# One transformer-like block on one core: both mixer gates and the attention branch's product by seven products of half sums, token-major

## The chip, the cores and the metric

The kernel runs on one core of a Trainium2 chip. A core has TensorE (PE, matrix products into PSUM), VectorE (DVE), ScalarE (ACT), GpSimd (POOL) and SyncE (SP, which here issues DMAs). The metric is the device time of one launch in microseconds; lower is better. The time of the kernel before is the median of three runs.

## The reference

One block over 512 tokens of width 2048, all in fp32. `u = rms_norm(x)`; `proj = u @ w_in` is split into the recurrence's input and gate, q, k, v, the indexer's queries, keys and weights, and two mixer gates of 2048 columns each.

```python
xc = causal_depthwise_conv(rx, conv_w[l], conv_b[l])
ya = rg_lru(xc, w_rg_r[l], b_rg_r[l], w_rg_i[l], b_rg_i[l], lru_lambda[l]) * jax.nn.gelu(rgate)
yb = dsa_sparse_attention(q, k, v, iq, ik, iw, slopes)      # 8 heads, 128 selected keys of 512
mixed = (jax.nn.sigmoid(gate_a) * (ya @ w_branch_rnn[l])
         + jax.nn.sigmoid(gate_b) * (yb @ w_branch_attn[l]))
h = h + mixed @ w_out[l]
h = h + jnp.square(jax.nn.relu(rms_norm(h, norm_mlp_g[l]) @ w_mlp_up[l])) @ w_mlp_down[l]
```

`rg_lru` makes two sigmoid gates r and i from block-diagonal products, a = exp(-8 r softplus(-lambda)), and scans h = a h + sqrt(1 - a^2) i xc along the tokens. `ya` has 1024 channels, `yb` 1024. w_in has 2048 rows, w_branch_rnn and w_branch_attn 1024, w_out 2048.

## The kernel before

Every product is made from two parts of each operand: hi (a cast to fp32r, ACT) and lo (the rest, DVE), and three matmuls: hi times hi, hi times lo, lo times hi (`products`, L1905). Weights come in units of 1 MB (4 chunks of 128 rows by 512 columns) into two `raw` slots (SP), ACT casts a unit into `whi[slot]` (`hi`, L743), DVE makes `wlo[slot]` (L1250), and PE multiplies it: 4 quarters of 12 matmuls, 48 in all. `next_hi` and `next_lo` stand at the place of unit j and make the parts of unit j + 1; the cast can start when unit j - 1 has been multiplied, since it takes that unit's slot. Each engine has its own program in a fixed order, and semaphores tie them: `quarter` counts PE's quarters, `drained` the banks that were emptied, `lo_ready` the units that are ready.

The order of the stages on PE is: the normalised input u turned feature-major (`uhi`, `ulo`), 16 units IQRX (indexer queries and the recurrence's input, in two rounds i of 8 units; the first four of a round, j = 0 to 3, take 384 columns, and in the last four the index scores are made beside them: `idx_step` on PE, `relu_step` on ACT, scores on DVE), 8 units RG (the recurrence's gate, beside which DVE selects the keys), 16 units GA (gate A, feature-major, in a loop of four), 8 units WR (the recurrence's product), 8 units HD (the values), 16 units KQ (keys and queries of two heads at a time, with the attention of the pair before), 24 units GB (gate B, 16 units, and the attention branch's product, 8 units), 16 units WO (`w_out`), and the MLP. In the MLP both products are made by seven products of half sums instead of eight: token halves, row chunks taken alternately and column halves make three 2 by 2 matrices, `A11 B11, S1 T1, S2 T2, A12 B21, S3 T3, S4 B22, A22 T4`, each in two parts hf of 12 matmuls (down stage: `dhi`, `dlo` hold seven parts, L1183 and L1837; results are added to `hh` by DVE, L1762, or by ACT into `dn_tmp`, L1144, and POOL, L704).

The recurrence runs beside GA, one quarter of its channels per round of four units (46.4 us): DVE makes the convolution (L1396, L1401) in place of unit 0, the block-diagonal product (`lru_gates`) stands behind unit 1 on PE, ACT makes r, i, a, tanh (L863 to L870) and the root (L874), DVE the scan (L1427) and the product with the gate (L1430), ACT and DVE its parts (L877, L1433), and DVE `bdlo` (L1406). GA's results are copied to `mix` (L881), scaled by POOL (L645), put through the sigmoid (L849), multiplied by the recurrence's product (L1444); gate B and the branch's product are added at L1549 to L1565.

## Time and profile before

| | |
|---|---|
| median of 3 runs | 2568.51 us (2568.38 to 2568.74) |
| profiled execution, first to last instruction (span) | 2566.7 us |
| PE busy | 2550.2 us, 99% of the span |
| DVE, ACT, POOL busy | 1729.9, 1162.2, 437.8 us |
| PE's granted clock, mean | 0.999 of full speed |
| chain that ended last | PE 97%, DVE 1% |

The profiled execution has no time of its own beside its span; the median of the runs is 1.8 us above the span. A row of the page or of an answer names the line, the engine, what is written and read, the number of instructions, and their busy time. PE's matmuls overlap in the records: a 512-column matmul is shown as 390 ns long, while the next starts about 227 ns later, so PE's pace is read from counts in a stretch and not from busy time.

### The profile page before, as it was taken

What the parts mean: (1) busy time and instruction counts of PE and PEld (TensorE: products, weight loads), DVE (VectorE), ACT (ScalarE), POOL (GpSimd) and SP (SyncE); (2) the same over time, 40 slices, a digit from 0 to 9 for tenths busy, and PEclk for the clock granted to TensorE, in tenths of its full rate; (3) what the DMA queues carried; (4) which work ended last, traced back from release to release, by engine and by line L of the source; (5) the groups of instructions that cost most, each with busy time, mean ns of one, the idle gap of its engine ahead of it and who ended that gap; (6) DMA issues with size and microseconds to landing.
All of it is one profiled execution on the core that took longest, in us unless ns stands there. A gap on an engine that the chain in (4) does not pass through costs nothing.

```text
span 2566.7 us, 35536 instructions
## 1 busy us (share of the span) xinstructions
PE 2550.2 (99%) x13299; PEld 2199.0 (86%) x13299; DVE 1729.9 (67%) x1859; ACT 1162.2 (45%) x1455; POOL 437.8 (17%) x341
## 2 busy tenths in 40 slices
PE   9999999999999999999999999999999999999998
PEld 8888888888888888888889999999998888888886
DVE  5558765432355433342488888888888899999997
ACT  6332454411233322232366666566655555554545
POOL 1000121100000000000001211112111353443433
PEclk9999999999999999999999999999999999999999
DMA  5222233222322222234336655666568786545652
GB/s 196 85 99 96 84 100 100 96 86 97 99 82 82 66 99 98 98 115 151 130 119 202 207 184 188 205 205 199 184 195 322 278 245 246 180 168 213 239 213 83
DMA packets 244731, 393.53 MB, mean 153 GB/s; under 512 B 8848, under 2 KB 148720, under 8 KB 236848
## 3 DMA queue, kind: packets, MB, share of 16 engines
q1 hardware_dynamic: 238880, 378.17, 43.8%
q0 software_dynamic: 5520, 14.16, 2.1%
q8 instruction: 50, 0.82, 0.1%
q10 hardware_dynamic: 256, 0.18, 0.0%
q14 instruction: 25, 0.20, 0.0%
HBM read 325.24 MB, written 67.11 MB: 153 GB/s over the span
## 4 chain that ended last, share of the span: by engine, by line
PE 97%; DVE 1%; ACT 0%; POOL 0%; issue 0%; DMA 0%; ACTq 0%; DVEq 0%
PE stream L1910 16%; PE stream L1909 16%; PE stream L1911 16%; PE stream L2250 4%; PE stream L2252 4%; PE stream L2251 4%; PE aux L2250 4%; PE aux L2252 4%; PE aux L2251 4%; PE aux L2222 4%; PE stream L2222 3%; PE aux L2229 2%; PE aux L2227 2%; PE aux L2228 2%; PE stream L2229 2%; PE stream L2227 2%
## 5 line engine op out<-in xcount | busy, mean ns | idle before, releaser
L1250 DVE TENSOR_TENSOR wlo<-raw,whi 128x2048 fp32r<-128x2048 f32 x112 | 260.8, 2328 | 419.5 <-ACT whi L743 419.3
L743 ACT CAST whi<-raw 128x2048 fp32r<-128x2048 f32 x112 | 213.8, 1909 | 536.5 <-PE stream L1911 536.0
L1909 PE MATMUL stream<-uhi,whi 128*128 128x512 f32 (+1 forms) x1152 | 442.6, 384 | 0.0
L1910 PE MATMUL stream<-ulo,whi 128*128 128x512 f32 (+1 forms) x1152 | 441.5, 383 | 0.0
L1911 PE MATMUL stream<-uhi,wlo 128*128 128x512 f32 (+1 forms) x1152 | 441.4, 383 | 0.0
L704 POOL TENSOR_TENSOR hh<-hh,dn_tmp 128x512 f32<-128x512 f32 x112 | 220.7, 1991 | 328.0 <-ACT dn_tmp L1144 328.0
L1911 PEld LDWEIGHTS stream<-uhi,wlo 128*128 128x128 f32 x1152 | 216.2, 188 | 40.2
L1909 PEld LDWEIGHTS stream<-uhi,whi 128*128 128x128 f32 x1152 | 216.3, 188 | 39.3
L1910 PEld LDWEIGHTS stream<-ulo,whi 128*128 128x128 f32 x1152 | 216.3, 188 | 39.0
L1183 ACT CAST dhi<-d 128x1024 fp32r<-128x1024 f32 x160 | 167.7, 1053 | 164.1 <-PE aux L2252 99.4
L1837 DVE TENSOR_TENSOR dlo<-d,dhi 128x1024 fp32r<-128x1024 f32 x160 | 225.8, 1428 | 13.0 <-ACT dhi L1183 12.9
L2250 PE MATMUL stream<-dhi,dsum 128*128 128x512 f32 x448 | 174.5, 389 | 1.4 <-DVE hh L1762 0.9
L2252 PE MATMUL stream<-dhi,dsum 128*128 128x512 f32 x448 | 174.4, 389 | 0.2 <-issue 0.2
L2251 PE MATMUL stream<-dlo,dsum 128*128 128x512 f32 x448 | 174.3, 389 | 0.0
L2251 PE MATMUL aux<-dlo,dsum 128*128 128x512 f32 x448 | 174.3, 389 | 0.0
L2250 PE MATMUL aux<-dhi,dsum 128*128 128x512 f32 x448 | 174.3, 389 | 0.0
L2252 PE MATMUL aux<-dhi,dsum 128*128 128x512 f32 x448 | 174.3, 389 | 0.0
L660 POOL DMA_DIRECT2D h<-in_x x4 | 3.1, 771 | 776.7 <-DVE mix L1565 649.3
L1065 ACT CAST uwhi<-up_a 128x1024 fp32r<-128x1024 f32 x94 | 98.8, 1051 | 67.9 <-DVE up_a L1650 67.0
L1837 DVE TENSOR_TENSOR dlo<-dn_e,dhi 128x1024 fp32r<-128x1024 f32 x64 | 94.5, 1496 | 34.4 <-ACT dhi L1183 34.4
L1671 DVE TENSOR_TENSOR uwlo<-up_a,uwhi 128x1024 fp32r<-128x1024 f32 x94 | 114.2, 1215 | 0.0
L1671 DVE TENSOR_TENSOR uwlo<-up_b,uwhi 128x1024 fp32r<-128x1024 f32 x64 | 78.3, 1223 | 47.3 <-ACT uwhi L1065 47.3
(369 smaller groups left out, 6118.9 us busy)
## 6 DMA issues: line engine op xcount, KB each, us to landing
raw<-in_w_in SPq DMA_DIRECT2D x80, 1024.0 KB, 5.1
d<-in_w_mlp_down SPq DMA_DIRECT2D x64, 1024.0 KB, 8.3
dsum<-sums_d SPq DMA_DIRECT2D x56, 1024.0 KB, 11.8
up_b<-in_w_mlp_up SPq DMA_DIRECT2D x32, 1024.0 KB, 11.4
up_a<-in_w_mlp_up SPq DMA_DIRECT2D x32, 1024.0 KB, 9.8
sums_d<-hlo SPq DMA_DIRECT2D x32, 896.0 KB, 4.3
sums_d<-hhi SPq DMA_DIRECT2D x32, 896.0 KB, 7.3
raw<-in_w_out SPq DMA_DIRECT2D x16, 1024.0 KB, 5.1
```

The source lines that it names most:

```text
L704: pool.tensor_tensor(v, v, dn_tmp[r][:], ALU.add).then_inc(s.dn_p, 1)
L743: nc.scalar.copy(whi[slot][:, 0:width], raw[slot][:, 0:width]).then_inc(s.hi_ready, 1)
L1250: V.tensor_tensor(wlo[slot][:, 0:width], raw[slot][:, 0:width], whi[slot][:, 0:width].bitcast(F32), ALU.subtract).then_inc(s.lo_ready, 1)
L1671: V.tensor_tensor(uwlo[k][:], parts[j], uwhi[k][:].bitcast(F32), ALU.subtract).then_inc(s.up_lo, 1)
L1837: V.tensor_tensor(dlo[m % 7][:], parts[j], dhi[m % 7][:].bitcast(F32), ALU.subtract).then_inc(s.dn_lo, 1)
L1909: T.matmul(dst, ah, bh, start=first and k == 0, stop=False)
L1910: T.matmul(dst, ah, bl, start=False, stop=False)
L1911: ins = T.matmul(dst, al, bh, start=False, stop=last and k == n - 1)
L2222: ins = T.matmul(both(q), wh, both_parts(q, j), start=opens and q == 0, stop=q == KP - 1, skip_group_check=True)
L2250: T.matmul(dst, sh, wh, start=opens and i == 0, stop=False, skip_group_check=not opens)
L2251: T.matmul(dst, sh, wl, start=False, stop=False, skip_group_check=not opens)
L2252: ins = T.matmul(dst, sl, wh, start=False, stop=i == 3, skip_group_check=not opens)
```

## The change

PE no longer multiplies GA and GB. The order of the units is IQRX, RG, HD, KQ, WR, then ten gate steps, then WO. In the steps `st` 0 to 3 are gate A (two groups g of 1024 input rows, for two halves n of 1024 columns), 4 and 5 the attention branch's product, 6 to 9 gate B; each has the seven products in 14 parts m, of 12 matmuls each, with sums of tokens stationary and 512 weight columns moving. Weight sums are made on DVE (8 additions of 128x1024 a step), hi parts on ACT, lo parts on DVE, in a ring of five buffers (`GATE_RING`). Results are scattered into `acc_g` and `acc_r` (512 columns at a time, 14 pairs of halves): of the group that opens a sum, products 0, 1, 2, 6 by ACT (`gate_out`) and the rest by DVE (`gate_sum`); of the other group all by DVE.

The sums of tokens of u are made during IQRX: POOL adds the parts and makes four differences (`ur`, `us`), ACT and DVE split them (`ushi`, `uslo`, `u_sums_hi`, `u_sums_lo`, one of eight pairs k at each of the units 4 to 11), and POOL writes them to DRAM (`usum_d`); SP reads them back before the steps. The same is done with yb during WR (`ysum_d`, four pairs p of two heads; ACT and DVE wait for the spill of the pair before).

The recurrence (quarters i, `lru_*`) stands beside the values: one quarter per two HD units, the last one in the first KQ round. Some of it changes engines: the first tap and a^2 go to ACT, the product with the gate and `bdlo` to POOL; the values are now emptied by ACT (L1122 of the changed kernel) and not by DVE. WR is token-major, its four results go to `acc_r`; `rx`, `yahi` lose the 4 columns of padding.

Gate A's half n is multiplied by POOL (128x2048 at a time), written to DRAM (`mixa_d`), and added back to the attention half by an accumulating DMA of 1 MB from POOL's queue. The mixed rows are then turned feature-major on PE (`turn_mix`: 16 chunks, 64 transposes of 128x128), positions 0 to 7 within step 9, 8 to 15 within the first WO units, where ACT and DVE make `mhi` and `mlo`.

ACT's order in the index part, second round, before: the casts of the weight units 1 to 4 and then of the next one. `whi_51`, `whi_52` are the two slots; `iq` the queries' parts.

```order
L743 CAST whi_52<-raw_50 128x2048
L743 CAST whi_51<-raw_49 128x2048
L743 CAST whi_52<-raw_50 128x2048
L825 CAST iq<-stream 64x384 x8
L743 CAST whi_51<-raw_49 128x2048
```

The same place in the changed kernel; `ushi` are the split token sums.

```order
L942 CAST whi_52<-raw_50 128x2048
L1018 CAST ushi<-us 128x1024
L942 CAST whi_51<-raw_49 128x2048
L1018 CAST ushi<-us 128x1024
L942 CAST whi_52<-raw_50 128x2048
L1030 CAST iq<-stream 64x384 x8
L1018 CAST ushi<-us 128x1024
L942 CAST whi_51<-raw_49 128x2048
```

A cast of token sums now stands behind each cast of a weight unit, and the queries' casts have one behind them.

ACT's order beside the recurrence before, one round of gate A from its fourth unit's cast: `bdhi`, `yahi` parts for the block-diagonal product, `lru_*` the recurrence, `mix` gate A.

```order
L743 CAST whi_52<-raw_50 128x2048
L857 CAST bdhi<-bd 128x512
L860 CAST yahi<-lru_xc 128x512 x2
L863 ACTIVATE lru_rr<-aux,par 128x512 x2
L865 ACTIVATE lru_ii<-aux,par 128x512 x2
L868 ACT_TABLE_LOAD
L868 ACTIVATE lru_aa<-lru_rr,sp_t 128x512 x2
L870 ACTIVATE lru_th<-lru_rr,sp_t 128x512 x2
L743 CAST whi_51<-raw_49 128x2048
L874 ACT_TABLE_LOAD
L874 ACTIVATE lru_rr<-lru_th 128x512 x2
L877 CAST yahi<-lru_xc 128x512 x2
```

The changed kernel, from the exponentials of quarter 0 to the first tap of quarter 2 (`xc_80`, `xc_81` are the two convolution buffers, `vv` the values):

```order
L1088 ACTIVATE lru_aa<-lru_rr,sp_t 128x512 x2
L1091 ACTIVATE lru_th<-lru_rr,sp_t 128x512 x2
L1094 ACTIVATE lru_rr<-lru_aa 128x512 x2
L1099 ACT_TABLE_LOAD
L1099 ACTIVATE lru_rr<-lru_th 128x512 x2
L1069 CAST bdhi<-bd 128x512
L1072 CAST yahi<-xc_81 128x512 x2
L942 CAST whi_52<-raw_50 128x2048
L1104 CAST yahi<-xc_80 128x512 x2
L1122 ACTIVATE vv<-stream,small 128x4x128 x4
L942 CAST whi_51<-raw_49 128x2048
L1063 ACTIVATE xc_80<-rx,par 128x512 x2
```

The root of one quarter, the parts of the next one, a weight cast, the parts of the first quarter's result, and the four evictions of the values now stand in one row on ACT.

POOL's order between the recurrence's gate and the second block-diagonal load, before:

```order
L640 TENSOR_TENSOR rg<-rg,rs_b 128x512 x8
L615 DMA bd<-in_w_rg_r 64x64 x2
L615 DMA bd<-in_w_rg_i 64x64 x2
L615 DMA bd<-in_w_rg_r 64x64 x2
L615 DMA bd<-in_w_rg_i 64x64 x2
L645 TENSOR_TENSOR mix<-mix,rs_b 128x512 x4
```

and in the changed kernel:

```order
L800 TENSOR_TENSOR rg<-rg,rs_b 128x512 x8
L804 TENSOR_TENSOR bdlo<-bd,bdhi 128x512
L744 DMA bd<-in_w_rg_r 64x64 x2
L744 DMA bd<-in_w_rg_i 64x64 x2
L744 DMA bd<-in_w_rg_r 64x64 x2
L744 DMA bd<-in_w_rg_i 64x64 x2
L810 TENSOR_TENSOR xc_80<-lru_th,rg 128x512 x2
L804 TENSOR_TENSOR bdlo<-bd,bdhi 128x512
```

`bdlo` is now POOL's, and that of the next quarter stands behind the product with the gate of the quarter before.

The diff, cut to its core:

```diff
-LRU_DVE = ["conv0", "conv1", "conv2", "conv3", "asq", "var", "gated", "u", "scan", "y", "lo"]
-LRU_ACT = ["r", "i", "a", "th", "mult", "hi"]
+LRU_DVE = ["var", "gated", "u", "scan", "lo"]
+LRU_ACT = ["r", "i", "a", "th", "asq", "mult", "hi"]
...
+GATE_STEPS = 10
+GATE_RING = 5
...
+def gate_step(st):
+    if st in (4, 5):
+        return "attn", 0, st - 4
+    return ("gate_a", st // 2, st % 2) if st < 4 else ("gate_b", (st - 6) // 2, st % 2)
...
+            pool.tensor_tensor(ur[:], uhi[:, 2 * k:2 * k + 2].bitcast(F32), ulo[:, 2 * k:2 * k + 2].bitcast(F32),
+                               ALU.add).then_inc(s.tok_add, 1)
+            pool.wait_ge(s.tok_add, 5 * k + 1)
+            a11, a21, a12, a22 = ur[:, 0, 0:HALF], ur[:, 0, HALF:S], ur[:, 1, 0:HALF], ur[:, 1, HALF:S]
+            pool.tensor_tensor(us[:, 0], a21, a22, ALU.subtract).then_inc(s.tok_add, 1)
+            pool.tensor_tensor(us[:, 2], a11, a21, ALU.subtract).then_inc(s.tok_add, 1)
...
+            pool.wait_ge(s.tok_lo, k + 1)
+            for c, v in enumerate((ushi, uslo)):
+                for q, e in ((S1, 0), (S3, 2)):
+                    pool.dma_start(usum_d[k // 4, q:q + 2, :, c, k % 4].rearrange("q p n -> p q n"),
+                                   v[:, e:e + 2].bitcast(F32)).then_inc(s.tok_sp, 16)
...
+        def lru_pool(i):
+            pool.wait_ge(s.lru_hi, 3 * i + 1)
+            pool.tensor_tensor(bdlo[:], bd[:], bdhi[:].bitcast(F32), ALU.subtract).then_inc(s.bd_lo, 1)
+
+        def lru_out(i):
+            for j in range(2):
+                pool.wait_ge(s.rg_gelu, 2 * i + j + 1)
+                pool.wait_ge(s.lru_v, lru_dve(i, "scan", j))
+                pool.tensor_tensor(xcs[i % 2][:, j], lru["th"][:, j], rg[:, 2 * i + j], ALU.mult).then_inc(s.lru_y, 1)
+
+        lru_pool(0)
+        for i in range(4):
+            if i < 3:
+                pool.wait_ge(s.bd_lo, i + 1)
+                load_bd(i + 1)
+            lru_out(i)
+            if i < 3:
+                lru_pool(i + 1)
...
+            for e, b in enumerate((2 * n + 1, 2 * n)):
+                pool.wait_ge(s.gate_sig, 2 * n + e + 1)
+                pool.tensor_tensor(acc_r[b][:], acc_r[b][:], acc_g[b][:], ALU.mult).then_inc(s.gate_mul, 1)
+            pool.wait_ge(s.gate_mul, 2 * n + 2)
+            for b in (2 * n + 1, 2 * n):
+                pool.dma_start(mixa_d[b], acc_r[b][:]).then_inc(s.ga_spl[n], 16)
+
+        for k, b in enumerate((1, 0, 3, 2)):
+            if k < 2:
+                pool.wait_ge(s.gate_sig, 4 + k + 1)
+                pool.tensor_tensor(acc_r[b][:], acc_r[b][:], acc_g[b][:], ALU.mult).then_inc(s.gate_mul, 1)
+            pool.wait_ge(s.gate_mul, 4 + k + 1)
+            pool.wait_ge(s.ga_spl[b // 2], 32)
+            pool.dma_start(acc_r[b][:], mixa_d[b], accum_op=ALU.add).then_inc(s.mix_acc[b], 16)
...
+        def u_sums_hi(k):
+            act.wait_ge(s.tok_add, 5 * k + 5)
+            if k:
+                act.wait_ge(s.tok_sp, 64 * k)
+            nc.scalar.copy(ushi[:], us[:]).then_inc(s.tok_hi, 1)
...
+        lru_first(0)
+        for i in range(2):
+            for j in range(4):
+                v = 4 * i + j
+                next_hi(U_HD, 4, i, j)
+                if v == 0:
+                    lru_parts(0)
+                elif v % 2 == 0:
+                    lru_first(v // 2)
+                    lru_gate(v // 2 - 1)
+                    lru_mult(v // 2 - 1)
+                    lru_parts(v // 2)
+                elif v > 1:
+                    lru_hi_out(v // 2 - 1)
+            for t in range(TT):
+                act.wait_ge(s.quarter, 4 * (U_HD + 3 + 4 * i) + t + 1)
...
+        def gate_act(st):
+            for m in range(14):
+                j, hf = m // 2, m % 2
+                act.wait_ge(s.gt_mm, 14 * st + m + 1)
+                if st == 0 and m == 0:
+                    act.wait_ge(s.quarter, 4 * (U_WR + 7))
+                if st == 0 and m == 1:
+                    act.wait_ge(s.tok_sp, U_SPILLS + 32 * 4)
+                parts = gate_parts(hf)[4]
+                if j == 0:
+                    act.wait_ge(s.gt_b11, 16 * st + 16)
+                elif j == 3:
+                    act.wait_ge(s.b21_in, 16 * st + 16)
+                elif j == 5:
+                    act.wait_ge(s.b22_in, 16 * st + 16)
+                else:
+                    act.wait_ge(s.half_add, 8 * st + {1: 0, 2: 2, 4: 4, 6: 6}[j] + hf + 1)
+                nc.scalar.copy(ghi[(14 * st + m) % GATE_RING][:], parts[j]).then_inc(s.half_hi, 1)
+                if m == 4 and st and opens_sums(st - 1):
+                    gate_out(st - 1, 6)
+                if m in (6, 8, 10) and opens_sums(st):
+                    gate_out(st, (m - 6) // 2)
+                if st in (3, 4, 9) and m in (5, 7):
+                    gate_sigmoid(st - 1, m == 5)
...
+        for v in range(8):
+            next_lo(U_HD, 4, v // 4, v % 4)
+            k = v // 2
+            if v % 2 == 0:
+                if k >= 2:
+                    lru_out_lo(k - 2)
+                lru_conv(k)
+                if k:
+                    lru_var(k - 1)
+            else:
+                lru_low(k)
+                if k:
+                    lru_scan(k - 1)
...
+                if st and m in (0, 2):
+                    gate_sum(st - 1, 4 + m // 2)
+                if st and m == 4 and not opens_sums(st - 1):
+                    gate_sum(st - 1, 6)
+                if m == 12 or m in (6, 8, 10) and not opens_sums(st):
+                    gate_sum(st, (m - 6) // 2)
+                if j == 0:
+                    dve.wait_ge(s.gt_b11, 16 * st + 16)
+                    dve.wait_ge(s.gt_b12, 16 * st + 16)
+                    if st:
+                        dve.wait_ge(s.half_lo, 14 * st - 14 + 13 + hf)
+                    add(0, ge[hf][:], b11, b12)
+                if j == 1:
+                    dve.wait_ge(s.b22_in, 16 * st + 16)
+                    dve.wait_ge(s.half_lo, 14 * st + 1 + hf)
+                    add(1, b11, ge[hf][:], b22)
+                if j == 2:
+                    add(2, b12, b12, b22)
+                if j == 3:
+                    dve.wait_ge(s.b21_in, 16 * st + 16)
+                    dve.wait_ge(s.half_lo, 14 * st + 3 + hf)
+                    add(3, ge[hf][:], b11, b21)
+                k = (14 * st + m) % GATE_RING
+                dve.wait_ge(s.half_hi, 14 * st + m + 1)
+                V.tensor_tensor(glo[k][:], parts[j], ghi[k][:].bitcast(F32), ALU.subtract).then_inc(s.half_lo, 1)
...
+        def lru_gates(i):
+            pe.wait_ge(s.bd_lo, i + 1)
+            if i:
+                pe.wait_ge(s.lru_a, lru_act(i - 1, "i", 1))
+            for j in range(2):
+                pe.wait_ge(s.lru_lo, 2 * i + j + 1)
+                for gate in range(2):
+                    ins = products(aux[2 * j + gate][:], [(bdhi[:, j, gate], bdlo[:, j, gate],
+                                                           yahi[:, 2 * i + j], xclo[:, j])], True, True)
+                ins.then_inc(s.lru_mm, 1)
...
+        def gate_pe(st):
+            for m in range(14):
+                j, hf = m // 2, m % 2
+                pe.wait_ge(s.half_lo, 14 * st + m + 1)
+                if hf == 0:
+                    pe.wait_ge(s.sums_in[j], 16 * (st // 2) + 16)
+                    if j == 0 and st >= 2:
+                        pe.wait_ge(s.gt_r[6], 2 * st - 2)
+                    if j == 1 and st:
+                        pe.wait_ge(s.gt_r[5], 2 * st)
+                    if j == 2:
+                        pe.wait_ge(s.gt_r[0], 2 * st + 2)
+                    if j == 3 and st:
+                        pe.wait_ge(s.gt_r[3], 2 * st)
+                    if j == 4:
+                        pe.wait_ge(s.gt_r[2], 2 * st + 2)
+                    if j == 5:
+                        pe.wait_ge(s.gt_r[1], 2 * st + 2)
+                    if j == 6:
+                        pe.wait_ge(s.gt_r[4], 2 * st + 2)
+                for r in range(2):
+                    ins = gate_rows(st, j, r, hf)
+                ins.then_inc(s.gt_mm, 1)
+                if st == GATE_STEPS - 1:
+                    turn_mix({9: (0, 1, 2), 11: (3, 4, 5), 13: (6, 7)}.get(m, ()))
```

## Rows read from the trace of the kernel before

**Rows 1.** Page, section 1: busy time, share and instructions of PE.

```profile
PE 2550.2 (99%) x13299; PEld 2199.0 (86%) x13299; DVE 1729.9 (67%) x1859; ACT 1162.2 (45%) x1455; POOL 437.8 (17%) x341
```

**Rows 2.** Windows: us; busy and instructions of PE, PEld, DVE, ACT, POOL; PEclk, DMA share, GB/s.

```profile
482.60:549.41 66.81, 66.81 (x290) 54.07 (x289) 21.78 (x18) 11.46 (x7) 0.00 (x0) 1.00 0.28 94
560.55:647.64 87.09, 87.09 (x386) 72.07 (x385) 24.15 (x17) 15.28 (x8) 0.00 (x0) 1.00 0.30 97
2071.77:2109.71 37.94, 37.94 (x169) 31.38 (x168) 35.42 (x29) 19.36 (x22) 20.27 (x12) 1.00 1.06 340
```

**Rows 3.** Chain of waits: start, us, what, on PE; eight transposes.

```profile
716.67 0.87 PE stream L2114 x8
```

**Rows 4.** Timeline of ACT, index part: start, us, line, op, count, idle before.

```profile
121.92 1.91 ACT L743 CAST whi<-raw 128x2048 fp32r<-128x2048 f32 x1 [6.43 <-PE stream L1911]
...
130.24 1.91 ACT L743 CAST whi<-raw 128x2048 fp32r<-128x2048 f32 x1 [6.41 <-PE stream L1911]
...
140.58 0.97 ACT L825 CAST iq<-stream 64x384 fp32r<-64x384 f32 x2
```

**Rows 5.** Groups of POOL by shape: busy us, mean ns, idle before.

```profile
L670 POOL TENSOR_TENSOR hs<-hs 128x256 f32<-128x256 f32 x32 | 56.6, 1768 | 0.0
...
L672 POOL TENSOR_TENSOR hs<-hs 128x256 f32<-128x256 f32 x32 | 23.7, 740 | 2.5
...
L725 POOL TENSOR_TENSOR hh<-hh,gfin 128x1024 f32<-128x1024 f32 x4 | 9.5, 2416 | 2.4 <-issue 2.4
...
L663 POOL DMA_DIRECT2D h_d<-h x4 | 3.0, 760 | 45.6 <-DVE h L1617 45.6
...
L640 POOL TENSOR_TENSOR rg<-rg,rs_b 128x512 f32<-128x512 f32 x8 | 12.4, 1552 | 238.4 <-ACT rg L841 238.4
```

**Rows 6.** Timeline of ACT beside the recurrence, second round.

```profile
343.31 1.91 ACT L743 CAST whi<-raw 128x2048 fp32r<-128x2048 f32 x1 [5.03 <-PE stream L1911]
...
345.64 1.14 ACT L860 CAST yahi<-lru_xc 128x512 fp32r<-128x512 f32 x2
...
357.51 1.26 ACT L865 ACTIVATE lru_ii<-aux,par 128x512 f32<-128x512 f32 x2
...
358.79 1.28 ACT L868 ACT_TABLE_LOAD   x1
...
361.33 1.32 ACT L870 ACTIVATE lru_th<-lru_rr,sp_t 128x512 f32<-128x512 f32 x2
...
365.77 1.15 ACT L874 ACTIVATE lru_rr<-lru_th 128x512 f32<-128x512 f32 x2
```

**Rows 7.** Timeline of DVE beside the recurrence, second round.

```profile
338.95 4.05 DVE L1401 SCALAR_TENSOR_TENSOR lru_xc<-rx,par,lru_xc 128x512 f32<-128x512 f32 x6
...
345.25 2.29 DVE L1250 TENSOR_TENSOR wlo<-raw,whi 128x2048 fp32r<-128x2048 f32 x1 [2.25 <-ACT whi L743]
...
366.70 1.28 DVE L1420 TENSOR_TENSOR lru_ii<-lru_ii,lru_xc 128x512 f32<-128x512 f32 x2
...
369.10 2.33 DVE L1427 TENSOR_TENSOR_SCAN lru_th<-lru_aa,lru_ii 128x512 f32<-128x512 f32 x2
```

**Rows 8.** Page, section 6: issues, KB each, median us to landing.

```profile
sums_d<-hhi SPq DMA_DIRECT2D x32, 896.0 KB, 7.3
```

**Rows 9.** Timeline of DVE, down stage.

```profile
2060.09 2.31 DVE L1837 TENSOR_TENSOR dlo<-d,dhi 128x1024 fp32r<-128x1024 f32 x1
...
2063.46 1.21 DVE L1837 TENSOR_TENSOR dlo<-d,dhi 128x1024 fp32r<-128x1024 f32 x1
...
2064.59 1.40 DVE L1762 SCALAR_TENSOR_TENSOR hh<-stream,small,hh 128x512 f32<-128x512 f32 x2
```

**Rows 10.** Timeline of POOL, down stage.

```profile
2056.72 4.59 POOL L704 TENSOR_TENSOR hh<-hh,dn_tmp 128x512 f32<-128x512 f32 x2 [1.01 <-ACT dn_tmp L1144]
```

**Rows 11.** Line 682, the accumulating DMAs of 512 KB.

```profile
DMA to landing us min/median/max: 7.7/12.1/18.3
```

**Rows 12.** Groups of DVE by shape: busy us, mean ns of one, idle before.

```profile
L1837 DVE TENSOR_TENSOR dlo<-d,dhi 128x1024 fp32r<-128x1024 f32 x160 | 225.8, 1428 | 13.0 <-ACT dhi L1183 12.9
```

840 lines of the change are left out of this document (543 added, 297 removed).

## The prediction

> **What bounds the kernel now.** I read the page's first section, then windows over single stages, then the timelines of ACT, DVE and POOL. PE is busy for 99% of the span [rows 1], so the time is PE's count of matmuls at its pace plus what PE waits. Six units of the recurrence's product take 66.81 us, eight units of values 87.09 and a step of half sums 37.94 [rows 2]: 11.14, 10.89 and 37.94 us for 48, 48 and 168 matmuls. PE's granted clock is 1.00 in all three, the upper of its levels. In the half-sum step DVE is busy for 35.42 of 37.94 us; beside plain units for about a quarter. So a saving on PE is certain only if DVE, ACT and POOL, given new work in fixed orders, keep up. I therefore price PE first and then each place where PE could stand.
>
> **PE's work.** GA, GB and the branch's product are 40 units of 10.89 us, 435.4 us. Ten steps at 37.94 are 379.4: **−56.0 us** (A). WR was 8 units at 11.14, with four columns of padding; token-major at 10.89 it gives **−2.0** (B; 0 to −2). The turning is 64 transposes; eight take 0.87 [rows 3], so **+7.0** (C).
>
> **Token sums of u, second round of the index part** (D). One unit with 384 columns is 8.32 us (121.92 to 130.24 [rows 4]). The pairs of sums come from POOL: one addition of 1024 columns (2.42), four differences of 256 columns at 0.74 to 1.77, and the pair's four DMA issues of 0.76 [rows 5], which stand behind ACT's and DVE's parts (about 1.05 and 1.2, estimates from the forms of 128x1024 at [rows 9] and of 2048 at [rows 4]). The cycle of a pair is 3.05 + 2.4 + 3.8 + 1.05 + 1.2 = 11.5 us, with differences near 0.95, against units of 8.32: POOL falls 3.2 us behind in each. ACT waits for POOL in front of the next unit's cast (order of ACT, index part), so the delay reaches PE once the slack ahead of a cast (6.41 less a half-sum cast of about 1) is spent: near the third and fourth unit of the round by 2.9 and 3.1, and by 1.4 more for the queries' parts. **+7.5**; with fast differences 3, with slow ones and all four units 14.
>
> **The recurrence beside the values** (E). Here is the largest doubt. Before, a quarter had a round of four units; now two units and its own block-diagonal product (12 matmuls, 2.7 us at 48 in 10.89): 24.5 us. Its chain crosses engines. ACT, from the gates' results: first tap 1.2, two gates on two halves 2.5, three table loads 3.8, exponential and tanh 2.6, squares and root 2.4 (forms of 1.26, 1.28, 1.32 and 1.15 [rows 6]); then the next quarter's parts 1.7 (1.14 of it at 345.64), and a weight cast of 1.9 in between. DVE: the unit's lo 2.29, low part 1.3, gated and u 2.5 (1.28 for two), scan 2.33 [rows 7]. POOL: the product, 1.55 for 512 columns [rows 5], and behind it `bdlo` of the next quarter, about 1.3; that is what PE's next block-diagonal product waits for (order of POOL). Counted in us from the first value unit:
> ACT starts on quarter 0 at 21.8 (two units), and is through the root and the parts at 37.8. Cast, lo, low part, two products and the scans end at 47.8; POOL's product 49.9, `bdlo` 51.2. PE wants it after four units and one product, at 46.2: wait 5.0. ACT comes to the next quarter after the parts of the result and four evictions (2.5) at 53.0; with 19.0 of ACT and 10 of DVE and then POOL, `bdlo` is there at 85.4, wanted at 75.7: 9.7. The third is wanted at 110.0 and there at 117.2: 7.2. The last quarter's result, which closes in the first head round, comes 3.3 late. Sum **+25.3**. Lower end: only the first wait is real, the rest overlaps better than counted, 5; upper end 31, if each quarter's chain takes the 24.5 plus the 4.59 that two POOL operations take beside a busy DVE [rows 10] instead of 3.1.
>
> **The sums of yb beside WR** (F). ACT and DVE wait for the spill of the pair before; 896 KB land in 7.3 us [rows 8]. With the parts the cycle is 11 to 13, the unit 10.89: **+1.5** (0 to 5).
>
> **Start of the gate steps** (G). The ring's first parts need the last unit's buffer drained: last eviction 0.6, cast 1.05, lo 1.2: **+3.0** (2 to 5).
>
> **Inside the steps** (H). Before, the down step had 14 lo parts, 8 weight additions and 7 results. Steps 2, 3, 8 and 9 now have 14 lo parts, 8 additions and 14 results: 22 × 1.21 + 14 × 0.70 = 36.4 us (1.21 and half of 1.40 [rows 9]) of 37.94. It fits, with nothing left. The other steps have 6 results: 30.8. What can break it is POOL: an lo part took 2.31 us in one case and 1.21 in the next [rows 9], the first while POOL still added. POOL multiplies 128x2048 at a time in steps 3, 4 and 9, about 4 × 2.3 = 9 us each, and each puts some 4.5 on DVE's own list. The ring holds five, so a late piece of about 2.7 us is forgiven; 1.8 are not, in steps 3 and 9: **+3.6** (0 to 12).
> The Trainium skill, in GPSIMD Engine Reference, section Key points, says that POOL contends with VectorE instructions in a two-port mode or with two SBUF inputs; the pair 2.31 and 1.21 agrees for the lo parts. By that rule the results, which have one input in PSUM, would go free of it; no row here shows it, and H would be about 2 us instead of 3.6.
>
> **The tail** (I). The mixed halves are added back by DMAs of 1 MB. An accumulating DMA of 512 KB took 7.7 to 18.3 us, median 12.1 [rows 11]; I take the 1 MB ones at its median to 18, from which the halves turned first are late by **+2** (0 to 8).
> The Trainium skill, DMA: Bandwidth & Descriptors, section Anatomy of one DMA — SWDGE (gpsimd) path, gives 2.0 us plus bytes over 436 GB/s, an estimate of 4.4 us for 1 MB. The median of 12.1 for half of that speaks against it for the accumulating kind; by the rule the tail would wait for nothing, and the sum be 2 us lower.
>
> **Sum.** −56.0 − 2.0 + 7.0 + 7.5 + 25.3 + 1.5 + 3.0 + 3.6 + 2.0 = −8.1 us on the span of 2566.7: 2558.6. The profiled run's span is 1.8 us below the median of the runs, so the forecast is **2560.5 us**. A change of 0.2%, 5.1 us, is about what a measurement of this kernel tells from none.
>
> **Rivals.**
> *First, the recurrence is covered.* If the later quarters overlap (DVE's `var` and scans done beside ACT's root, POOL's product running under the cast), only the first 5 us stay of E, and the sum is −28: 2540 us. For it: every engine but PE has half its time free there (ACT 15.28, DVE 24.15 of 87.09 [rows 2]). Against it: the order is fixed and each quarter passes ACT, DVE and POOL in turn; a free engine doesn't shorten a chain.
> *Second, slower: DVE bounds the gate steps.* The lo parts of the down stage are 1.43 us in the mean [rows 12], not 1.21. If that mean holds for parts and additions beside the mixers' work, a heavy step is 22 × 1.43 + 14 × 0.70 = 41.3 us, 3.3 over PE in each of four, 13 us; and at each of the ten starts the results of the step before, two at a time, come in a row with the block additions that open the ring: some 1.2 us each, 12 more. From −8 that is +17: 2585. It decides from the point at which DVE's list for a step is over 37.94 us. For it: 35.42 already with 7 results. Against it: the down step with that mean still ran at PE's pace, and most of POOL's additions there are gone.
> *Third, the gain is eaten without DVE.* POOL's pairs run at 14 us instead of 11.5 and fall behind in all of the second round (+14 instead of 7.5), with two more us at G and F each: about 2569, no change. For it: 1.77 us for a 256-column difference on POOL [rows 5]. Against it: 0.74 for the same form elsewhere.
>
> **How the numbers follow.** Chances: forecast 0.50, first rival 0.17, second 0.18, third 0.15. The likeliest's own range is 2549 to 2572 (E from 15 to 31 with H and D at their ends). For eight in ten I cut into both outer cases: 2543 to 2580. Faster by over 0.2%: 0.35 of the forecast's half and all of the first, 0.52. Slower by over 0.2%: 0.16 of the second, 0.05 of the third, 0.03 of the forecast, 0.24. Within: 0.24.
>
> **What the profile after will show.** A: PE's instructions about 13299 − 240 + 64 and steps of 37.94 us between POOL's mixes. E: PE idle ahead of the block-diagonal products, ended by `bdlo` on POOL, growing from about 5 to 10 us and the values' stretch over 120 us. D: PE idle in the second index round, chain through POOL's `us` and ACT. G: one idle piece of 3 us as the steps begin. H: idle in steps 3 and 9 only, ended by DVE's lo parts, which are longer there. I am wrong if PE waits under 10 us in the values, if idle time appears at most steps' starts, or if heavy steps are longer than light ones without POOL at work.

## The result, and the profile after

The changed kernel takes 2579.1 us, the median of 4 runs (2578.24 to 2582.11), against 2568.53 before: a ratio of 1.0043 (95% interval 1.0031 to 1.0055), slower by 10.6 us where 8 us less were forecast. The profiled execution has a span of 2580.3 us, 13.6 more than before, and that is the figure explained below. It is the slowest of the four runs, 3.0 us above their median, while the profiled run of before stands at its median; so some 3 us of the 13.6 are of this one execution.

The page's first section of the changed kernel, busy us, share of the span and instructions of each engine:

```profile
PE 2518.6 (98%) x13123; PEld 2172.4 (84%) x13123; DVE 1953.6 (76%) x2054; ACT 1278.7 (50%) x1622; POOL 578.4 (22%) x458
```

Against [rows 1], PE is busy for 31.6 us less, but its span is longer: it idles 61.7 us instead of 16.5. For what it idles, the view of waits of PE tells (engine and tile <- releaser, line: us in total, times, longest):

```profile
PE aux L2288 <- POOL bdlo L804: 19.0, 3, 8.1
PE stream L2288 <- DVE wlo L1558: 9.0, 2, 5.3
PE stream L2564 <- DVE glo L1922: 7.4, 3, 3.1
PE stream L2288 <- DVE iq L1662: 3.2, 1, 3.2
PE aux L2564 <- DVE acc_g L1885: 3.1, 2, 1.5
PE stream L2288 <- DVE vf L1779: 2.5, 1, 2.5
PE stream L2683 <- ACT snap_P L1427: 2.4, 1, 2.4
```

The first row is the block-diagonal products of quarters 1 to 3, the sixth the heads (the attention's stage that follows the values): the forecast's E. The second is one unit of the index part (3.7, D) and the last of the recurrence's product (5.28, F); the fourth is D too. The third and fifth are the gate steps (G and H). The seventh stands at the start of the MLP and was in no term. The second thing to read is PEclk, in windows that begin where a wait ends (us; busy and instructions of PE, PEld, DVE, ACT, POOL; PEclk, DMA share, GB/s):

```profile
142.20:144.00 1.80, 1.71 (x7) 1.71 (x8) 0.03 (x1) 0.00 (x0) 1.78 (x3) 0.68 0.79 231
...
348.00:350.00 2.00, 1.91 (x5) 1.52 (x6) 0.00 (x0) 2.00 (x5) 0.66 (x3) 0.50 0.00 0
...
382.20:384.20 2.00, 1.91 (x5) 1.53 (x6) 0.71 (x1) 1.26 (x1) 1.71 (x5) 0.50 0.03 8
...
443.80:447.80 4.00, 3.93 (x17) 3.30 (x18) 2.79 (x4) 2.97 (x3) 0.00 (x0) 1.00 0.01 4
...
717.40:721.40 4.00, 3.92 (x9) 3.17 (x10) 1.15 (x2) 0.00 (x0) 0.00 (x0) 0.50 0.99 329
734.30:738.30 4.00, 3.94 (x9) 3.17 (x10) 4.00 (x4) 2.19 (x3) 0.00 (x0) 0.50 1.01 422
...
870.00:874.00 4.00, 3.95 (x17) 3.30 (x18) 4.00 (x5) 0.90 (x1) 0.37 (x1) 1.00 0.95 383
...
1323.90:1327.90 4.00, 3.96 (x21) 3.99 (x22) 3.93 (x4) 4.00 (x7) 0.00 (x0) 0.58 1.07 349
```

After waits of 3.70, 5.17, 8.06, 5.28 and 3.08 us the granted clock is down, to 0.50 of full speed (the lower of the two levels) for at least part of the window: 9 matmuls stand in 4 us, 0.43 us apart. After the waits of 2.55 (at 443.87) and 2.11 us (at 870.05) it is 1.00, and 17 matmuls stand in 4 us. After the wait of 2.41 us at the start of the MLP (the last window) it is 0.58. I summed, over the matmuls behind each wait, the distance to the next one above 0.227 us: the seven waits of 3.08 us and more are followed by losses of 1.61, 1.60, 1.48, 1.45, 2.51, 2.73 and 2.81 us, **14.2 us** together. What is lost behind the 2.41 us isn't in this sum, since other forms of matmul stand there. The forecast had no term for this; before, no wait of PE was longer than 1.6 us, and the clock in [rows 2] is 1.00 throughout.

### The profile page after: what moved, and what is told of

The parts are those of the page before. It is cut to its first block, busy times and chain, and to the rows that moved or that the text cites. A ratio compares the mean times of both kernels' runs of the same rounds, so it can differ in the third digit from the quotient of the medians.

```text
span 2580.3 us, 35447 instructions
## 1 busy us (share of the span) xinstructions
PE 2518.6 (98%) x13123; PEld 2172.4 (84%) x13123; DVE 1953.6 (76%) x2054; ACT 1278.7 (50%) x1622; POOL 578.4 (22%) x458
## 4 chain that ended last, share of the span: by engine, by line
PE 85%; DVE 6%; issue 3%; ACT 3%; DMA 2%; POOL 1%; ACTq 0%; POOLq 0%; DVEq 0%
PE stream L2288 8%; PE stream L2289 7%; PE stream L2290 7%; PE stream L2706 4%; PE stream L2708 4%; PE stream L2707 4%; PE aux L2708 4%; PE aux L2707 4%; PE aux L2706 4%; PE aux L2678 3%; PE stream L2678 3%; PE aux L2685 2%; PE aux L2683 2%; PE aux L2684 2%; PE stream L2683 2%
## 5 line engine op out<-in xcount | busy, mean ns | idle before, releaser
L1558 DVE TENSOR_TENSOR wlo<-raw,whi 128x2048 fp32r<-128x2048 f32 x72 | 171.6, 2384 | 199.3 <-ACT whi L942 199.3
L2288 PE MATMUL stream<-uhi,whi 128*128 128x512 f32 (+1 forms) x640 | 244.8, 383 | 9.4 <-DVE wlo L1558 3.7
L2289 PE MATMUL stream<-ulo,whi 128*128 128x512 f32 (+1 forms) x640 | 243.6, 381 | 0.0
L2290 PE MATMUL stream<-uhi,wlo 128*128 128x512 f32 (+1 forms) x640 | 243.4, 380 | 0.0
L942 ACT CAST whi<-raw 128x2048 fp32r<-128x2048 f32 x72 | 137.4, 1908 | 213.3 <-PE stream L2290 213.3
L2216 DVE TENSOR_TENSOR dlo<-d,dhi 128x1024 fp32r<-128x1024 f32 x160 | 228.2, 1444 | 11.5 <-ACT dhi L1491 11.4
L1922 DVE TENSOR_TENSOR glo<-g,ghi 128x1024 fp32r<-128x1024 f32 x100 | 138.9, 1395 | 45.0 <-ACT ghi L1265 44.9
L1265 ACT CAST ghi<-g 128x1024 fp32r<-128x1024 f32 x100 | 105.3, 1054 | 128.8 <-PE aux L2566 83.1
L2288 PEld LDWEIGHTS stream<-uhi,whi 128*128 128x128 f32 x640 | 121.1, 189 | 30.0 <-issue 6.4
L2290 PEld LDWEIGHTS stream<-uhi,wlo 128*128 128x128 f32 x640 | 121.0, 189 | 20.4
L2289 PEld LDWEIGHTS stream<-ulo,whi 128*128 128x128 f32 x640 | 121.1, 189 | 19.2
## 6 DMA issues: line engine op xcount, KB each, us to landing
up_b<-in_w_mlp_up SPq DMA_DIRECT2D x32, 1024.0 KB, 11.4
```

Of the source, the lines that this page charges most:

```text
L1558: V.tensor_tensor(wlo[slot][:, 0:width], raw[slot][:, 0:width], whi[slot][:, 0:width].bitcast(F32), ALU.subtract).then_inc(s.lo_ready, 1)
L1922: V.tensor_tensor(glo[k][:], parts[j], ghi[k][:].bitcast(F32), ALU.subtract).then_inc(s.half_lo, 1)
L2216: V.tensor_tensor(dlo[m % 7][:], parts[j], dhi[m % 7][:].bitcast(F32), ALU.subtract).then_inc(s.half_lo, 1)
L2288: T.matmul(dst, ah, bh, start=first and k == 0, stop=False)
L2289: T.matmul(dst, ah, bl, start=False, stop=False)
L2290: ins = T.matmul(dst, al, bh, start=False, stop=last and k == n - 1)
```

## The experiments

Each time is the median of its runs, and each ratio is to the kernel before, measured beside it (2568.8 us in the first four, 2568.8 in the next three, 2568.6 in the last three).

### e1: waits put into the kernel before

```diff
+        for v, n in enumerate((256, 512, 768, 1024, 1280, 1536, 2048, 3072)):
+            pool.wait_ge(s.quarter, 4 * (U_HD + v) + 2)
+            pool.tensor_tensor(idle[:, 0:n], idle[:, 0:n], idle[:, 0:n], ALU.subtract).then_inc(s.held, 1)
...
+                if held is not None and t == 2:
+                    pe.wait_ge(s.held, held)
```

> The kernel before, in which PE waits once in the middle of each of the eight units of values for a POOL subtraction of 256, 512, 768, 1024, 1280, 1536, 2048 and 3072 columns, begun when PE ends the quarter ahead. By 2.41 us for 1024 columns the eight waits are about 0.9, 1.5, 2.1, 2.7, 3.3, 3.9, 5.1 and 7.5 us, 27 in all. First theory (a wait of about 3 us and more makes PE's granted clock fall for the matmuls after it, as after the seven waits of 3.08 us and more of the changed kernel): the last four are followed by matmuls 0.43 us apart, at 1.5 to 2.8 us lost each, the first four by none; 27 + 9 = 36 us more, 2604. Second theory (the slow matmuls of the changed kernel come from what else runs there, the sums' transfers or POOL): no slow matmuls here, 27 us more, 2595.

2598.1 us (2595.5 to 2600.2), ratio 1.0116 (1.0100 to 1.0133). The eight waits are 0.91, 1.17, 1.60, 2.03, 2.55, 2.88, 3.73 and 5.44 us in the trace, 20.3 in all: shorter than planned, so that only two of them, not four, are over 3 us. Windows behind the last three (columns as above):

```profile
633.10:637.10 4.00, 3.94 (x17) 3.29 (x18) 0.00 (x0) 0.00 (x0) 0.01 (x1) 1.00 0.17 58
648.00:652.00 4.00, 3.93 (x10) 3.12 (x11) 0.00 (x0) 0.00 (x0) 0.01 (x1) 0.57 0.00 0
666.20:670.20 4.00, 3.91 (x9) 3.13 (x10) 0.00 (x0) 0.00 (x0) 0.04 (x1) 0.50 0.00 0
```

With DVE, ACT and POOL idle and hardly a transfer under way, the clock falls behind the waits of 3.73 and 5.44 us, with 1.7 and 2.9 us lost, and not behind 2.88 and less. The profiled run's span is 27.0 us over that of before: 20.3 us of waits, 4.6 of slow matmuls behind the last two, some 0.1 behind each of the others, and 1.5 that stay open. So the slow matmuls come with the waits alone, and the second theory falls; the forecast of 36 us more was too high, because the waits came out shorter and only two of them were followed by slow matmuls. The four runs spread over 4.7 us, where the kernel before spreads over 1.1.

### e2: bdlo ahead of the product with the gate, on POOL

```diff
-            lru_out(i)
             if i < 3:
                 lru_pool(i + 1)
+            lru_out(i)
```

> The changed kernel with bdlo of the next quarter ahead of the product with the gate on POOL. First theory (the four waits beside the values come from the ring ACT, DVE, POOL, ACT of the recurrence, in which quarter i + 1 starts on ACT only after the product of quarter i; bdlo is only the last link): the first wait of 5.2 us goes, the others come back behind the lo part of the convolution's output, the heads start when they did; 0 to 3 us less than the changed kernel, 2576 to 2579. Second theory (POOL's order makes the waits): the three waits at the block-diagonal product go from 19.0 to under 5 us and their slow matmuls with them, 18 us less, 2561.

2579.2 us, ratio 1.0043 (1.0027 to 1.0060): nothing is gained. `bdlo` is gone from PE's waits, and this stands there instead:

```profile
PE aux L2288 <- DVE xclo L1721: 9.0, 2, 5.6
PE stream L2564 <- DVE glo L1922: 7.4, 3, 3.1
PE stream L2288 <- ACT vv L1122: 7.1, 2, 4.5
PE stream L2288 <- DVE vf L1779: 3.7, 1, 3.7
```

19.8 us of the 21.5 beside the values have moved to other releasers, `xclo`, the evictions of the values and the heads. The releaser named in a row of waits was only the last link of a chain. This run also shows the clock's other side: its wait at the first gate step is 3.08 us long, as in the changed kernel, and

```profile
733.50:737.50 4.00, 3.90 (x17) 3.30 (x18) 4.00 (x4) 2.20 (x3) 0.00 (x0) 1.00 1.02 424
```

the clock stays at 1.00 there, where it was 0.50. In e3, below, it is the reverse at the heads: a wait of 2.55 us, as in the changed kernel, but

```profile
434.20:436.20 2.00, 1.93 (x5) 1.57 (x6) 1.82 (x3) 1.98 (x3) 0.00 (x0) 0.50 0.04 8
```

So between about 2 and 3 us the same wait is sometimes paid for at the lower level and sometimes not.

### e3: the sums of u beside the long units

```diff
-                if 4 <= 8 * i + j < 12:
-                    u_sums_hi(8 * i + j - 4)
+                if j >= 4:
+                    u_sums_hi(4 * i + j - 4)
```

(and the same for the lo parts on DVE)

> The changed kernel with the eight pairs of token sums of u beside the four long units of each round (13 us each) instead of beside eight units in a row, four of which take 8.3 us. First theory (the pair's cycle of 11.0 to 13.4 us against 8.3 is the whole of the excess in the index part): the waits of 3.70 and 3.17 us go and the 3.2 us lost at the lower clock with them, 10 us less, 2569. Rival (the selection on DVE or the transfers take over in the second round's end): the pairs delay the lo parts or rx there, a new wait of 3 to 6 us at the gate's units, 2573 to 2576.

2570.9 us, ratio 1.0007 (0.9997 to 1.0017): 8.2 us less than the changed kernel; the index part has no wait but those that were there before. In the changed kernel ACT's timeline there was (start, us, line, what, idle before):

```profile
124.73 1.05 ACT L1018 CAST ushi<-us 128x1024 fp32r<-128x1024 f32 x1 [9.18 <-DMA usum_d<-uslo]
125.69 1.91 ACT L942 CAST whi<-raw 128x2048 fp32r<-128x2048 f32 x1
135.72 1.05 ACT L1018 CAST ushi<-us 128x1024 fp32r<-128x1024 f32 x1 [8.13 <-POOL us L784]
136.68 1.90 ACT L942 CAST whi<-raw 128x2048 fp32r<-128x2048 f32 x1
```

The cast of a weight unit, due every 8.3 us, stood behind a cast of sums that came every 11 to 13 us (124.73, 135.72, the next at 149.16), as the forecast had it.

### e4: the last weight unit ahead of the last sums of yb

```diff
         rnn_out(2)
+        rnn_hi(7)
         y_sums_hi(3)
-        rnn_hi(7)
+        act.wait_ge(s.quarter, 4 * (U_WR + 7))
+        act.wait_ge(s.gt_b11, 16)
+        nc.scalar.copy(ghi[0][:], gate_parts(0)[4][0]).then_inc(s.half_hi, 1)
         rnn_out(3)
```

(the same order for the lo parts on DVE; `gate_act` then leaves out the hi part that is made here)

> The changed kernel in which ACT and DVE make the last weight unit of the recurrence's product ahead of the last pair of sums of yb, and ACT the first hi part of the gate steps ahead of the last evictions. First theory (the 5.28 us are ACT waiting for a spill to land in front of a cast, the 3.08 us the hi part behind the evictions): both waits go or fall under 1.5 us, and 5.5 us at the lower clock with them; 12 us less, 2567. Rival (the steps' first parts are late for their weights or the ring's room, since the spill lands as late as before): the first wait goes, a wait of 3 to 6 us stays at the first or second part of step 0; 3 to 8 us less, 2571 to 2576.

2574.9 us, ratio 1.0026 (1.0015 to 1.0036): 4.2 us less than the changed kernel. The wait of 5.28 us is gone, but the steps' start waits 3.92 us (3.08 before), for another releaser, with 2.9 us at the lower clock behind it:

```profile
PE stream L2569 <- DMA gsum<-usum_d: 3.9, 1, 3.9
```

The rival has it: the first theory's second half was wrong. The sums of product 0 share their place with those of yb, and their load waits until the last pair has landed in DRAM.

### e5: the recurrence's links reordered

POOL as in e2, and:

```diff
 # DVE; in even units next_lo stays first
-            next_lo(U_HD, 4, v // 4, v % 4)
...
 # DVE, odd units
-                lru_low(k)
                 if k:
                     lru_scan(k - 1)
+                lru_low(k)
+                next_lo(U_HD, 4, v // 4, v % 4)
...
 # DVE, first round of the heads
+                lru_scan(3)
             next_lo(U_KQ, 4, p, 1)
             if not lag:
-                lru_scan(3)
...
 # ACT: the result's parts move from the odd units, ahead of the evictions, into the next even unit
+                    if v >= 4:
+                        lru_hi_out(v // 2 - 2)
                     lru_first(v // 2)
```

> The changed kernel with the recurrence's links reordered: bdlo ahead of the product on POOL, the scan and the low part ahead of the unit's lo part on DVE, the evictions of the values and the weight cast ahead of the parts of the result on ACT. First theory (the ring of ACT 11.2 us, scan 3.6, product and parts 3 is 18 to 21 us, and fits the 24.5 us of two units once no unit part stands inside it): the waits of 21.5 us beside the values fall under 5, and the 5.4 us of slow matmuls with them; 20 to 25 us less than the changed kernel, 2554 to 2559. Rival (the ring doesn't fit two units in any order, since the lo parts of the weight units are now late instead): waits of 3 to 5 us at the value units, at most 8 us less, 2571.

2555.5 us, ratio 0.9951 (0.9934 to 0.9968): 23.6 us less than the changed kernel. Beside the values PE waits 0.95 us in all. The stretch of the values with the four block-diagonal products, in the changed kernel and here:

```profile
296.50:419.40 122.90, 103.92 (x434) 84.65 (x433) 66.14 (x75) 74.61 (x95) 30.10 (x35) 0.93 0.23 72
...
296.80:396.30 99.50, 98.55 (x434) 80.77 (x432) 74.17 (x75) 72.44 (x93) 32.07 (x35) 1.00 0.25 79
```

The same 434 matmuls take 99.5 us instead of 122.9, and the clock is 1.00 instead of 0.93 in the mean.

### e8, e9, e10: which of the three orders it was

e8 is e5 with ACT's order of the changed kernel, e9 is e5 with DVE's, e10 is e5 with POOL's.

> The reordered recurrence of e5_chain with DVE's new order and POOL's, and ACT's order as in the changed kernel (parts of the result in the odd units, ahead of the evictions). If the ring's late link is DVE (the scan behind a unit's lo part, some 7 us), the product of quarter 0 comes at 338 instead of 345 us and everything behind it is in time: the waits beside the values stay under 3 us, 2555 to 2558, as e5_chain. Rival (both orders are needed): the evictions still stand behind the parts of the result, two waits of 2.6 and 4.5 us at the evictions as in e2_swap, 2565 or more.

> The same with ACT's new order and POOL's, and DVE's order as in the changed kernel (unit's lo part and low part ahead of the scan). If DVE's order is the late link: ACT still starts quarter 1 near 350.5 instead of 356; the low part of quarter 2 is late by 2 us and of quarter 3 by 3, the heads by up to 2: 4 to 8 us over e5_chain, 2559 to 2563. If ACT's order is the late link, as e5_chain, 2555.

> e5_chain with POOL's order as in the changed kernel, bdlo behind the product with the gate. If POOL's order costs nothing once the scan is early (product of quarter 0 done near 340, bdlo 341, PE wants it at 343): as e5_chain within its interval, 2555 to 2557. Rival (the chain's last link matters in its own right): waits of 1 to 3 us at each block-diagonal product, 2558 to 2562.

2555.9, 2570.4 and 2555.4 us; ratios 0.9950 (0.9933 to 0.9967), 1.0007 (0.9997 to 1.0017) and 0.9947 (0.9930 to 0.9963). Without DVE's order the other two are worth 8.7 us; with it, ACT's can be taken back (e8) or POOL's (e10), and all of the gain stays. In e10 PE waits for `bdlo` once, for 1.22 us. DVE's order with neither of the two was not run. The rival of e8 (both orders are needed) and that of e10 fall. e9 was forecast at 2559 to 2563 and is slower: its waits are 1.30, 4.55 and, at the heads, 7.60 us, so the link by DVE costs more in the last quarter than I had counted (its scan of quarter 3 stands behind a unit's lo part again, too). What the order does, in DVE's timeline of the changed kernel, from the end of the first quarter's squares:

```profile
330.03 1.29 DVE L1727 SCALAR_TENSOR_TENSOR lru_th<-lru_rr,lru_th 128x512 f32<-128x512 f32 x2 [3.30 <-ACT lru_rr L1094]
336.38 2.29 DVE L1558 TENSOR_TENSOR wlo<-raw,whi 128x2048 fp32r<-128x2048 f32 x1 [5.06 <-ACT whi L942]
338.59 1.28 DVE L1721 TENSOR_TENSOR xclo<-xc,yahi 128x512 fp32r<-128x512 f32 x2
...
342.20 2.33 DVE L1740 TENSOR_TENSOR_SCAN lru_th<-lru_aa,lru_ii 128x512 f32<-128x512 f32 x2
```

and in e8, with DVE's order and POOL's:

```profile
330.61 1.29 DVE L1727 SCALAR_TENSOR_TENSOR lru_th<-lru_rr,lru_th 128x512 f32<-128x512 f32 x2 [3.30 <-ACT lru_rr L1094]
...
334.29 3.44 DVE L1740 TENSOR_TENSOR_SCAN lru_th<-lru_aa,lru_ii 128x512 f32<-128x512 f32 x2
337.66 3.41 DVE L1721 TENSOR_TENSOR xclo<-xc,yahi 128x512 fp32r<-128x512 f32 x2
340.99 2.28 DVE L1558 TENSOR_TENSOR wlo<-raw,whi 128x2048 fp32r<-128x2048 f32 x1
```

In the first, DVE sits idle for 5.06 us for the cast of a weight unit that PE takes up only after the block-diagonal product, past 350, and then makes its lo part, with the scan queued behind both; in the second the scan starts 3.7 us after the first row instead of 12.2. POOL's product, ACT's parts of it and its next gates all follow the scan. (The two scans and the two low parts take 3.44 and 3.41 us there instead of 2.33 and 1.28; POOL makes `bdlo` and the product beside them, from 334.16 to 340.5. The order gains more than that costs.)

### e6: without POOL's products of the mixer halves

```diff
-                pool.tensor_tensor(acc_r[b][:], acc_r[b][:], acc_g[b][:], ALU.mult).then_inc(s.gate_mul, 1)
+                pool.tensor_tensor(acc_r[b][:, 0, 0:16], acc_r[b][:, 0, 0:16], acc_g[b][:, 0, 0:16], ALU.mult).then_inc(s.gate_mul, 1)
```

> The changed kernel with POOL's products of the mixer halves made for 16 of 2048 columns only, the rest left out. First theory (POOL's 128x2048 products hold up DVE's additions and lo parts, 1.2 us to 4.8 and 5.6, and the ring of five doesn't cover that): the waits of 2.11, 1.53, 0.52, 2.17 and 1.54 us within the steps go; 7 to 9 us less with the matmuls after them, 2571. Rival (DVE's list in the steps with 14 results is too long by itself): the waits in step 3 and 9 stay, 0 to 2 us less, 2578.

2572.1 us, ratio 1.0013 (1.0004 to 1.0023): 7.0 us less, and no wait is left within the steps. The kernel leaves the products out, so this prices them and is no version to use. In the changed kernel DVE's timeline of step 3 shows why:

```profile
857.22 1.21 DVE L1922 TENSOR_TENSOR glo<-g,ghi 128x1024 fp32r<-128x1024 f32 x1
858.36 1.40 DVE L1885 SCALAR_TENSOR_TENSOR acc_g<-aux,small,acc_g 128x512 f32<-128x512 f32 x2
859.68 4.78 DVE L1896 TENSOR_TENSOR ge<-g,g 128x1024 f32<-128x1024 f32 x1
864.38 5.61 DVE L1922 TENSOR_TENSOR glo<-g,ghi 128x1024 fp32r<-128x1024 f32 x1
869.91 1.21 DVE L1896 TENSOR_TENSOR ge<-g,g 128x1024 f32<-128x1024 f32 x1
```

beside POOL's:

```profile
858.75 10.15 POOL L842 TENSOR_TENSOR acc_r<-acc_r,acc_g 128x2048 f32<-128x2048 f32 x2 [142.47 <-ACT acc_g L1246]
```

Two DVE operations of 1.21 us last 4.78 and 5.61 while POOL's two run, and return to 1.21 when they end. In step 4 the next two of POOL's products go the other way at first. DVE, which is without a gap from before 900 too:

```profile
906.49 1.22 DVE L1896 TENSOR_TENSOR ge<-g,g 128x1024 f32<-128x1024 f32 x1
907.62 3.49 DVE L1922 TENSOR_TENSOR glo<-g,ghi 128x1024 fp32r<-128x1024 f32 x3
911.33 10.90 DVE L1922 TENSOR_TENSOR glo<-g,ghi 128x1024 fp32r<-128x1024 f32 x2 [0.22 <-ACT ghi L1265]
```

and POOL:

```profile
900.35 20.80 POOL L842 TENSOR_TENSOR acc_r<-acc_r,acc_g 128x2048 f32<-128x2048 f32 x2 [29.98 <-ACT acc_g L1246]
```

From 900 to 911 DVE's operations follow each other without a gap and keep their 1.2 us, and POOL's product, begun at 900.35, lasts 15.2 us where the first of step 3 lasted 4.6; at DVE's first gap of 0.22 us it is POOL's turn, and DVE's next two take 10.90. The Trainium skill, SBUF — State Buffer, section SBUF: two separate sides, says it so: the pair of ports that the two share is locked by whichever instruction starts first, until it ends. The rows of step 3 agree; in step 4 a DVE operation was already running at 900.35, and those behind it kept the pair until the first gap.

### e7: all of it together

e5, e3 and e4, and on SP one weight load of the first step behind the landing of the third pair of sums of yb, so that this pair's spill, for which the casts of the last pair wait, meets less traffic.

```diff
         gate_load(g12, s.gt_b12, 0, 0, 1)
+        sp.wait_ge(s.tok_sp, U_SPILLS + 32 * 3)
         gate_load(g22, s.b22_in, 0, 1, 1)
-        sp.wait_ge(s.tok_sp, 64 * KP)
```

(the line taken out asks for less than the new one)

> The changed kernel with the recurrence's links reordered as in the run before last, the sums of u beside the long units, the last weight unit and the first hi part ahead of the last pair of sums of yb, and one weight load of the first step behind the landing of the third pair. If waits and the slow matmuls behind them are all that the changed kernel lost, the parts add: 23 + 8 + 10 less, 2538, and 30 us less than the kernel before. If what is taken off in one place comes back in the next (the transfers at the start of the steps, the selection beside the gate), 2550 to 2560.

2533.1 us (2532.7 to 2534.1), ratio 0.9862 (0.9845 to 0.9878): 46.0 us less than the changed kernel and 35.7 less than the kernel before. PE's longest waits are these:

```profile
PE stream L2571 <- DVE glo L1929: 4.3, 2, 2.2
PE aux L2571 <- DVE acc_g L1892: 3.1, 2, 1.5
PE stream L2690 <- ACT snap_P L1433: 2.7, 1, 2.7
PE aux L2378 <- POOL ident L731: 1.6, 1, 1.6
PE stream L2571 <- DMA gsum<-usum_d: 1.5, 1, 1.5
```

None is as long as 3 us, the mean clock is back at 0.998, and the runs lie within 1.3 us of each other. The first two are what POOL's products cost (e6). The page's first row begins:

```profile
PE 2503.1 (99%) x13123; PEld 2161.4 (85%) x13123; DVE 1970.8 (78%) x2054; ACT 1278.8 (51%) x1622; POOL 586.9 (23%) x458
```

The two profiled spans differ by 49.3 us (2580.3 and 2531.0). PE idles 27.9 us instead of 61.7, 33.8 less, and the same 13123 matmuls are busy for 15.5 us less: for the most part the 14.2 us of the lower clock, seen from the other side. The parts give more together than one by one (23.6, 8.2 and 4.2 are 36.0, against 46.0, and against the 41 forecast). Most of the rest is at the start of the steps: the waits of 5.28 and 3.08 us and 5.5 us of slow matmuls behind them have become one wait of 1.51 us at a clock of 1.00, where e4 had kept one of 3.92. The third pair's spill, issued at 662.9 us, is waited for until 670.4, 7.4 us instead of 11.4. The held load was not run by itself, so its share in this stays open.

## Why the prediction was wrong

It said −8.1 us on the span; the measured difference is +13.6 (+10.6 between the medians). By its own terms, forecast and measured:

| term | forecast | measured |
|---|---|---|
| A, ten steps for 40 units | −56.0 | −54.6 (a free step is 38.08 us, first matmul to first matmul; so is one of the down stage before, and the window of 37.94 in [rows 2] was 0.14 short) |
| B, product token-major | −2.0 | no excess over 10.89 us a unit but its waits: −2.0 |
| C, 64 transposes | +7.0 | about +7.2 (3.7 in the `w_out` stage, 3.5 taken for step 9) |
| D, sums of u | +7.5 | 6.9 (3.70 + 3.17) |
| E, recurrence | +25.3 | 21.5 (5.17, 8.06, 5.75, 2.55) |
| F, sums of yb | +1.5 | 5.3 |
| G, start of the steps | +3.0 | 3.1 |
| H, within the steps | +3.6 | 7.9 (2.11, 1.53, 0.52, 2.17, 1.54) |
| I, tail | +2.0 | 0 |
| clock behind the waits | none | 14.2 |

**The step that failed** is the one between the waits and the sum: each wait was priced at its length alone. The waits D to I were forecast at 42.9 us and are 44.7 (so close partly by luck: more in F and H stands against less in E and I); what turned a small gain into a loss is the 14.2 us that PE needs more for the matmuls behind seven of them (e1 shows that such a loss comes with the wait and nothing else, e7 that it goes with the waits). At the 2 us that such a loss measures in the mean (14.2 over seven), the forecast's own waits would have carried 8 us for the four of E (3.3 to 9.7) and up to 14 with the three of about 3 us in D and G (2.9, 3.1 and 3.0), and −8 would have been 0 to +6. Without the 14.2 us the measured difference would be −0.6: no change. The Trainium skill, TensorE: Matmul & The Clock Gate, section Why this matters for your kernels, warns that long idle gaps between bursts of matmuls put PE back to its lower level. The windows above agree, and the forecast left this out. The rest of the 21.7 us between forecast and result is 3.4 in A, C and the sum of the waits, where 4.3 us more within the steps, 3.8 at the sums of yb and small differences stand against 3.8 less in E and 2 in the tail, and 4.1 us that I can't assign, of which 2.5 are in the MLP's first product (641.8 us long before, 644.3 after), where PE waits 0.9 us more and the clock is 0.93 in the first 23.5 us: the wait of 2.41 us and the lower clock behind it, the same step left out once more.

The prediction's own signs didn't cover this step: of what would have shown it wrong, nothing came (PE waits 21.5 us beside the values and not under 10, the steps' starts but the first are without a wait, and the heavy steps without POOL are as long as the light ones), and PE's 13123 instructions are as forecast.

**E was right in size and half right in cause.** The four waits were forecast at 5.0, 9.7, 7.2 and 3.3 us, and POOL was named as what PE waits for, because `bdlo` stands behind the product. PE does wait for it, but its order is worth nothing (e2, e10). The prediction's own chain held the true link, "DVE: the unit's lo 2.29, low part" ahead of the scan, and passed over it as duration, not as an order that can be changed. The ring itself fits two units: with the scan first the waits are 0.95 us in all (e5). So the first rival (the recurrence is covered) was right that the engines have the time, and wrong that this kernel's order lets them use it.

**D** was right in its mechanism (POOL's cycle of a pair against the short unit, e3) and nearly in size. **H**: the mechanism was right (POOL beside DVE's two-input operations, in steps 3 and 9, and hardly in 4), the size half. I took 4.5 us on DVE's list for each product, from [rows 9, 10]; the two of step 3 put 7.96 on it (4.78 + 5.61 less twice 1.21), so each costs 4.0; the ring's cover of 2.7 us is used once, and the second part and the result queued behind it come late too, which I didn't count. DVE's results, with one input in PSUM, stayed free of POOL, but the lower H of about 2 us that the prediction gave for that case is further off. The second rival (DVE bounds the steps) falls: steps 2 and 8, with 14 results and no product of POOL, are 38.08 us long, as the light ones. The third was added up 2 us too low (its own terms give 2571, not 2569); D came at 6.9 us and not at its 14. **F**: I set the cycle of a pair against the unit (11 to 13 to 10.89), but the third pair's spill met three weight loads and one of sums, 1 MB each, and the last pair's cast waited 9.32 us for its landing. **I**: the tail waits for nothing. The accumulating DMAs of 1 MB landed after 8.0 to 11.4 us, median 8.1, against the 12.1 to 18 that I took. The estimate of 4.4 us by the figure of the Trainium skill (DMA: Bandwidth & Descriptors, section Anatomy of one DMA — SWDGE (gpsimd) path) was too low, and that nothing waits, as the prediction concluded from it, came true by the slack ahead of the turning.

## What to carry to other kernels

Price an idle gap of the busiest engine not only at its length: in the changed kernel's trace each gap of 3 us or more cost 1.4 to 2.8 us on top, and gaps under 2 us 0.4 at most, so many short gaps are cheaper than a few long ones of the same sum. When a row of waits names a releaser, follow its engine's queue back to the first piece of work that stands ahead of it without being needed yet; swapping the last two links changed nothing, and with the scan moved ahead of lo parts that weren't needed yet it gave 23 us (e8). And a change that saves work on the bound engine is worth a second look at the fixed orders beside it before it is given up: the same seven products are 10.6 us slower, or with other orders around them 35.7 us faster, than what they replaced.
